# Latent attention: VectorE takes the residues of projections and rotary parts one step later, behind the next row maximum

## The reference

```
def mla(h, cos, sin, w_down, q_norm, w_uq, kv_norm, w_ukv, w_o):
    d = h @ w_down
    cq = rms_norm(d[..., :Q_LORA_RANK], q_norm)
    ckv = rms_norm(d[..., Q_LORA_RANK:Q_LORA_RANK + KV_LORA_RANK], kv_norm)
    k_rope = apply_rope(d[..., Q_LORA_RANK + KV_LORA_RANK:], cos, sin)
    q = (cq @ w_uq).reshape(B, S, N_HEADS, QK_HEAD_DIM)
    q_rope = apply_rope(q[..., QK_NOPE_DIM:], cos[:, :, None], sin[:, :, None])
    ...
    kv = (ckv @ w_ukv).reshape(B, S, N_HEADS, QK_NOPE_DIM + V_HEAD_DIM)
    ...
    o = causal_attention(q, k, v)
    return o.reshape(B, S, N_HEADS * V_HEAD_DIM) @ w_o
```

## Time and profile before

| | |
|---|---|
| runs | 1404.74, 1399.61, 1399.73 us |
| median | 1399.73 us |
| profiled execution, span from first to last instruction | 1397.3 us |
| PE busy | 1321.2 us (95%) |
| DVE busy | 794.2 us (57%) |
| ACT busy | 531.6 us (38%) |
| mean granted clock of PE | 0.984 |
| chain that ended last | PE 82%, DVE 11%, ACT 4% |

### The profile page before, as it was taken

One profiled execution on the slowest core, in us unless ns is written; L12 is line 12 of the kernel. 1 busy time (PEld: TensorE's weight loads), 2 busy tenths in 40 slices (PEclk: granted clock), 3 DMA queues, 4 the chain that ended last, 5 costly groups with the idle time before them and its releaser, 6 DMA issues.

```text
span 1397.3 us, 16364 instructions
## 1 busy us (share of the span) xinstructions
PE 1321.2 (95%) x6203; PEld 1094.2 (78%) x6203; DVE 794.2 (57%) x1112; ACT 531.6 (38%) x753; POOL 29.0 (2%) x32
## 2 busy tenths in 40 slices
PE   7899999999999888899999999999999899977997
PEld 6688888888877777788888888888887787765876
DVE  6744445444458775564544444455685578876554
ACT  5522233233334544433322232343233445555334
POOL 5000000000000000000000000000000000020000
PEclk9999999999999999999999999999999999988999
DMA  5222322222331100222232222325342110102321
GB/s 180 91 95 93 112 90 90 84 92 84 101 99 51 55 31 31 87 94 91 90 107 95 99 75 83 102 83 155 121 151 62 59 52 25 61 0 105 114 68 61
DMA packets 120888, 119.43 MB, mean 85 GB/s; under 512 B 13500, under 2 KB 117896, under 8 KB 120584
## 3 DMA queue, kind: packets, MB, share of 16 engines
q1 hardware_dynamic: 120784, 118.76, 26.4%
q10 hardware_dynamic: 56, 0.01, 0.0%
HBM read 114.57 MB, written 4.19 MB: 85 GB/s over the span
## 4 chain that ended last, share of the span: by engine, by line
PE 82%; DVE 11%; ACT 4%; issue 2%; DMA 1%; SPq 0%; DVEq 0%; ACTq 0%
PE psum L1743 25%; PE psum L1744 25%; PE psum L1745 25%; DVE w_lo L1089 2%; PE psum L2096 1%; ACT w_hi L628 1%; PE psum L2082 1%; PE psum L2068 1%; DVE xg_lo L1319 1%; DMA band<-in_c_band 1%; PE psum L1783 1%; PE psum L2172 0%; PE psum L2154 0%; DVE du L1420 0%; PE psum L2190 0%
## 5 line engine op out<-in xcount | busy, mean ns | idle before, releaser
L1743 PE MATMUL psum<-xg_hi,w_hi 128*128 128x512 f32 x1072 | 426.9, 398 | 3.9 <-DVE xg_lo L1657 2.9
L1745 PE MATMUL psum<-xg_hi,w_lo 128*128 128x512 f32 x1072 | 418.1, 390 | 0.0
L1744 PE MATMUL psum<-xg_lo,w_hi 128*128 128x512 f32 x1072 | 418.0, 390 | 0.0
L1743 PEld LDWEIGHTS psum<-xg_hi,w_hi 128*128 128x128 f32 x1072 | 201.9, 188 | 47.9 <-DVE xg_lo L1657 3.5
L1745 PEld LDWEIGHTS psum<-xg_hi,w_lo 128*128 128x128 f32 x1072 | 201.5, 188 | 42.6
L1744 PEld LDWEIGHTS psum<-xg_lo,w_hi 128*128 128x128 f32 x1072 | 201.9, 188 | 40.6 <-issue 1.4
L1206 DVE TENSOR_TENSOR w_lo<-w_raw,w_hi 128x2048 fp32r<-128x2048 f32 x42 | 96.3, 2292 | 152.6 <-ACT w_hi L707 152.6
L1230 DVE TENSOR_TENSOR w_lo<-w_raw,w_hi 128x2048 fp32r<-128x2048 f32 x32 | 73.4, 2293 | 115.9 <-ACT w_hi L726 115.9
L1743 PE MATMUL psum<-act_hi,w_hi 128*128 128x512 f32 x352 | 137.2, 390 | 0.0
L1744 PE MATMUL psum<-act_lo,w_hi 128*128 128x512 f32 x352 | 137.0, 389 | 0.0
L1745 PE MATMUL psum<-act_hi,w_lo 128*128 128x512 f32 x352 | 136.9, 389 | 0.0
(11 more groups left out here) (375 smaller groups left out, 1735.2 us busy)
## 6 DMA issues: line engine op xcount, KB each, us to landing
w_raw<-in_ffn_w_gate SPq DMA_DIRECT2D x22, 1024.0 KB, 5.0
w_raw<-in_ffn_w_up SPq DMA_DIRECT2D x22, 1024.0 KB, 5.0
w_raw<-in_w_in SPq DMA_DIRECT2D x16, 1024.0 KB, 5.5
w_raw<-in_ffn_w_down SPq DMA_DIRECT2D x16, 768.0 KB, 4.8
w_raw<-in_ffn_w_down SPq DMA_DIRECT2D x16, 640.0 KB, 4.5
w_raw<-in_mla_w_o SPq DMA_DIRECT2D x4, 1024.0 KB, 5.1
w_raw<-in_w_out SPq DMA_DIRECT2D x4, 1024.0 KB, 5.5
w_raw<-in_w_ple_gate SPq DMA_DIRECT2D x4, 1024.0 KB, 5.0
```

The costliest lines, as they stand in the source:

```text
L1743: pe.matmul(o, wh, xh, start=start, stop=False, skip_group_check=True)
L1744: pe.matmul(o, wh, xl, start=False, stop=False, skip_group_check=True)
L1745: return pe.matmul(o, wl, xh, start=False, stop=stop, skip_group_check=True)
```

## The change

On DVE the rotary residue and the treatment of the projections (residues, and the four multiplications of "u") no longer stand at the end of their own step. They are issued in the following step, between its row maximum and the normalising. The orders of PE, ACT, POOL and SP are as they were, and every semaphore wait and its count stay the same. The number of instructions does not change.

```diff
@@ -1369,15 +1369,17 @@
                     h, ii = divmod(s, NB)
                     if s < NB * HEADS:
                         row_max(s)
+                    if 0 < s < NB * HEADS:
+                        before = divmod(s - 1, NB)
+                        if rotary_head(*before) is not None:
+                            rotary(rotary_head(*before))
+                        for t in after_step(*before):
+                            proj(*t)
                     if 0 <= s - 1 < NB * HEADS:
                         normalise(s - 1)
                     if 0 <= s - 4 < NB * HEADS:
                         turned_lo(s - 4)
                     if s < NB * HEADS:
-                        if rotary_head(h, ii) is not None:
-                            rotary(rotary_head(h, ii))
-                        for t in after_step(h, ii):
-                            proj(*t)
                         if h % 2 == 0 and ii >= 1:
                             split_lo(FIRST["heads"] + 1 + h // 2, ii - 1)
```

## The result

The changed kernel takes 1412.24 us (median of 4 runs, 1410.57 to 1414.46) against 1399.67 us for the kernel before on the same chip (4 runs, 1396.58 to 1404.74): ratio 1.0088, 95% interval [1.0072, 1.0105]. It is 12.6 us slower; 1414 had been predicted, with 1406 to 1420 as the range. The profiled execution has a span of 1410.2 us, 12.9 more than before.

The account below looks back on a forecast made before the run. PE, busy 95%, was taken as the bound, so the change counts through its waits. 10.2 us plus 4 for the clock on the 1397.3 span gave 1411.5; the median lying 2.4 above, 1414 us, range 1406 to 1420.

Parts of the forecast that it names:

- The sum: Whole kernel: 10.2 us plus 4 us for the clock, 14.2 us on the span of 1397.3.
- kn0 before u: Head 3, step 13: PE starts u at 485.43 instead of 483.94, behind kn0's put-off residue, 1.5 us of new idle time.
- u before qn0, the output residue as a link: Head 3, step 14: qn0 4.4 us late behind output residue, row maximum and multiplications; without the output residue 0.9 us earlier.
- qn0 before the scores of head 4: End of head 3: the scores start at 498.5 instead of 493.79, making head 3 4.7 us longer.
- Heads 3 and 5 together: Each head 4.7 us longer by the loop, 9.4 in all, plus 4 us for a fall of PE's clock.
- The small terms: Other heads: 0.1 us for head 1, 0.1 each for heads 2, 4 and 6, 0.4 for head 7.
- The row maximum leads: Rival: row maxima fill DVE's 16.1 us of waiting for ACT, some 6 us faster, 1394 us; chance 0.05.
- Hidden: Rival: the latent attention stretch gives the lost time back through PE's 21 us of waits, 1400 us; chance 0.05.
- The loop without the clock: Rival: the loop over the banks as forecast, but PE keeps 2.4 GHz, 1410 us; chance 0.25.

Follow-up runs that it names:

- e5: Kernel before, with only the residues of kn0 and va in heads 3 and 5 put off to the next step; 1401.09 us, ratio 1.0009.
- e3: Changed kernel, but in heads 3 and 5 DVE's residue of the earlier head's output stands behind the moved u and vb; 1409.56 us, ratio to before 1.0066.
- e4: Changed kernel with 14 unused 512-column matmuls added on PE ahead of qn0 in each of heads 3 and 5; 1407.99 us, ratio to before 1.0054.
- e7: Kernel before, with only the rotary residue and qn0's residue in heads 3 and 5 put off to the next step; 1399.71 us, ratio 1.0001.
- e8: Kernel before, with only the rotary residue of heads 2, 4 and 6 moved behind the next row maximum; 1396.32 us, ratio 0.9974.
- e1: Kernel before, with the change made in heads 3 and 5 alone; 1410.63 us, ratio 1.0073.
- e6: Kernel before, with only u and vb in heads 3 and 5 put off to the next step; 1407.46 us, ratio 1.005.
- e2: Kernel before, with the change made in all heads but 3 and 5; 1398.94 us, ratio 0.9999.
- e10: Changed kernel with odd heads' projections listed kn0; va, u; qn0, vb instead of kn0, va; u, vb; qn0; 1403.81 us, ratio to before 1.0034.
- e9: e8, with DVE's residue of step 0's transposed probabilities taken at that step's end in heads 2 to 7; 1399.49 us, ratio to before 1.0.
- e11: e9 with the projection list of e10; 1400.7 us, ratio to before 1.0007.

## Why the prediction was right

**The sum.** 14.2 us were predicted on the span, 12.9 came; with the step from span to median, the forecast lay 1.8 us above the measured 1412.24. The mechanism forecast, a loop over the two banks and a fall of the clock behind its long gap, is the one that the runs show.

**kn0 before u, 1.5 us.** Right: from mask matmul to u 1.73 against 0.20 us, and e5, with this part alone, adds 1.5 a head. The wait that the profile lists there is 1.28 us and not 1.5, since PE has transposes between the mask matmul and u.

**u before qn0, the output residue as a link.** Right in size and mechanism. From u to qn0 8.27 us were predicted (485.43 to 493.70), 8.29 measured (485.09 to 493.38); the link by itself, put at 0.9, is 0.93 in e3. (The working gave the mask matmul of step 14 a length of 0.27 us; its row says 0.23. The 0.04 us change nothing.)

**qn0 before the scores of head 4.** About 4.8 us were predicted at full clock; e4 has 4.84. That the deferral of qn0 alone costs little (0.3) was not said, e7 shows it.

**Heads 3 and 5 together.** The prediction gave 9.4 us to the loop and 4 to the clock, e4 separates them as 9.1 and 4.0. The 4 us were a choice within 0 to 8, by the rows only; that it came out so exactly is in part luck, as the two heads lost 2.5 and 1.5. The Trainium skill ("TensorE: Matmul & The Clock Gate", Part 1) has the clock follow how busy TensorE has been recently, low by default and released by activity; e4, where the gap is filled and the clock stays at 1.00, agrees. The page warns of idle gaps; that the clock also fell behind waits of about 1 us with work between them, as in e7 and e8, is what the traces add.

**The small terms.** 0.8 us were predicted: head 1 has 0.21 (0.1 predicted), the even heads 0.11, 0.11 and 0.08 (0.1 each), head 7 and what follows 0.27 (0.4). The last is no clean measure, because the clock fell at other places of that stretch in each trace: with the old order in head 7 it lasts 35.55 us in the kernel before but 33.80 to 34.37 in e1, e5, e6 and e7, with the new one 35.82 and 35.75 in the changed kernel and e2 but 34.20 and 34.19 in e3 and e4. Missed was that DVE comes to head 3 and 5 a little earlier by the even heads' change, 0.2 us each (e2). The even heads' near zero was rightly called an exchange, but its two sides were not worked out; they are 0.8 us of loss and 0.7 of gain in PE's waits, and taking them apart led to e8, though not by the sum expected there.

**The rivals.** "The row maximum leads" said DVE's 16.1 us of waiting would be filled. They went, but for waits for PE, 29.4 us for scores in 16 places. A gain is there, but in one part only: 0.9 us a head in e8, where just the rotary residue of the even heads moves. The change as a whole loses 0.1 to 0.2 in each of heads 1, 2, 4 and 6, and with the list of e10 it still costs 3.5 us. "Hidden" fails as said: ACT and DVE moved along with PE. "The loop without the clock", 1410, is about the kernel of e4 (1407.99). What stays open is when exactly the clock falls: in the profiled executions it fell behind waits of 4.4 us six times of six (the changed kernel, e1, e6) and behind 1.95 to 2.2 us six times of six (e9, e11), but also behind about 1.1 in e8 (head 2) and behind 0.81 and 0.56 in e7 (head 5), and not in the same places elsewhere. The length of a wait does not decide it: each of the fourteen traces has a wait of 2.6 us before the output projection, and in the 5 us behind it the clock was 1.00 in eight of them (the kernel before and the changed one, e1 to e4, e10, e11) and 0.66 to 0.71 in the other six.

## What to carry to other kernels

To put an evacuation behind the next step's reduction is free only if the buffer that it frees is not wanted before that reduction can run. With two buffers in turn, list the uses in order and ask for each whether its predecessor by two now stands behind something that the waiting engine itself has just produced. A filled hole on a helper engine is worth what the bound engine's next wait shrinks by; e8 shows one such place worth 0.9 us, in a change that elsewhere cost 6 to 7 a head.

## What the hardware showed that was not expected

Gathering waits seems to cost clock. With the same work, two waits of 1.17 and 0.57 us left the clock at 1.00 (e8), and one of 1.96 was followed by 0.70 over the next 5 us, with 1.4 us more for each of two heads (e9). The profiled executions of e9 and e11 show this in six places of six; with the two waits apart, the clock fell behind them in 2 of 21 places (the kernel before in head 6, e7 in head 4). It is a tendency and no rule: four of e9's runs were as fast as e8, and one and the same wait of 2.6 us was followed by a fall in six traces of fourteen. And useless matmuls in a gap of 4.4 us paid back 4.25 us in two places (e4 against the changed kernel), so besides how long PE waits it is worth asking how the waits are spread.
